# Rotary partner rows by on-chip transfers, and the last projection computed by token rows

## The reference, cut to what matters

```python
for layer in range(DEPTH):
    h = h + 0.5 * rms_norm(swiglu(rms_norm(h, g[0]), ffn_w_in[layer, 0], ffn_w_out[layer, 0]), g[1])
    hn = rms_norm(h, g[2])
    m = attention_mixer(...) if layer % 2 == 0 else recurrent_mixer(...)
    h = h + rms_norm(m, g[3])
    h = h + 0.5 * rms_norm(swiglu(rms_norm(h, g[4]), ffn_w_in[layer, 1], ffn_w_out[layer, 1]), g[5])
return h[:, N_META:]

def apply_rope(x, cos, sin):      # per head, after its RMS norm with gain
    x1, x2 = x[..., :32], x[..., 32:]
    return jnp.concatenate([x1 * c - x2 * s, x1 * s + x2 * c], axis=-1)
```

## Time and profile before

| | us |
|---|---|
| median of the runs shown (3) | 1121.16 |
| lowest, highest | 1120.73, 1124.25 |
| the profiled execution's own time | 1124.99 |
| its span, first to last instruction | 1123.2 |
| TensorE busy with products in it | 1074.9 (96%) |
| VectorE, ScalarE, GpSimd busy | 716.9, 552.4, 117.7 |
| mean granted TensorE clock | 0.987 of full speed |

### The profile page before, as it was taken

How to read it: one execution, slowest core, us unless ns; L and a number is a source line. 1 busy time by engine, 2 the same in 40 slices (tenths; PEclk the granted TensorE clock), 3 DMA queues, 4 the chain that set the end, 5 groups by cost and what they waited for, 6 DMA issues and landing times.

```text
span 1123.2 us, 21352 instructions
## 1 busy us (share of the span) xinstructions
PE 1074.9 (96%) x8696; PEld 1046.3 (93%) x8696; DVE 716.9 (64%) x1012; ACT 552.4 (49%) x806; POOL 117.7 (10%) x103
## 2 busy tenths in 40 slices
PE   6999999998899999999999999999997699999998
PEld 5999999987669999999999999999897699999997
DVE  5766655475574766664467666545889967666542
ACT  4544454452575544435454534534587455444541
POOL 2000000033100200000020000000477310000000
PEclk9999999998999999999999999999998899999999
DMA  8565446625103255445645454557153163645541
GB/s 245 192 202 169 133 148 201 230 76 160 39 1 113 82 193 176 150 155 169 211 141 187 152 173 154 162 185 225 56 171 125 33 217 125 214 153 174 179 131 38
DMA packets 166464, 169.65 MB, mean 151 GB/s; under 512 B 3312, under 2 KB 165416, under 8 KB 166392
## 3 DMA queue, kind: packets, MB, share of 16 engines
q1 hardware_dynamic: 166088, 168.16, 46.6%
q0 software_dynamic: 96, 0.28, 0.1%
q10 hardware_dynamic: 208, 0.20, 0.1%
HBM read 167.30 MB, written 1.05 MB: 150 GB/s over the span
## 4 chain that ended last, share of the span: by engine, by line
PE 85%; DVE 11%; issue 2%; ACT 2%; DMA 1%; POOL 0%; SPq 0%; DVEq 0%
PE bank L365 25%; PE bank L367 24%; PE bank L366 24%; DVE wl L1090 2%; DVE h L1133 1%; PE bank L393 1%; PE flipped L582 1%; DVE gm L1386 1%; PE weighed L594 1%; DVE mg L1129 1%; DVE xl L1096 1%; PE bank L373 1%; ACT wh L735 1%; PE bank L486 1%; PE bank L384 1%
## 5 line engine op out<-in xcount | busy, mean ns | idle before, releaser
L1090 DVE TENSOR_TENSOR wl<-raw,wh 128x2048 fp32r<-128x2048 f32 (+2 forms) x178 | 366.3, 2078 | 177.2 <-ACT wh L735 176.8
L365 PE MATMUL bank<-xh,wl 128*128 128x272 f32 (+1 forms) x1552 | 451.1, 291 | 10.4 <-DVE xl L1391 7.9
L367 PE MATMUL bank<-xh,wh 128*128 128x272 f32 (+1 forms) x1552 | 448.4, 289 | 0.0
L366 PE MATMUL bank<-xl,wh 128*128 128x272 f32 (+1 forms) x1552 | 446.9, 288 | 0.0
L735 ACT ACTIVATE wh<-raw 128x2048 fp32r<-128x2048 f32 (+2 forms) x177 | 299.3, 1714 | 97.3 <-PE bank L367 97.3
L365 PEld LDWEIGHTS bank<-xh,wl 128*128 128x128 f32 x1552 | 295.4, 190 | 13.0 <-DVE xl L1391 8.1
L366 PEld LDWEIGHTS bank<-xl,wh 128*128 128x128 f32 x1552 | 295.3, 190 | 0.1
L367 PEld LDWEIGHTS bank<-xh,wh 128*128 128x128 f32 x1552 | 295.3, 190 | 0.0
L365 PE MATMUL bank<-ah,wl 128*128 128x272 f32 (+1 forms) x704 | 201.5, 286 | 0.0
L367 PE MATMUL bank<-ah,wh 128*128 128x272 f32 (+1 forms) x704 | 201.1, 286 | 0.0
L366 PE MATMUL bank<-al,wh 128*128 128x272 f32 (+1 forms) x704 | 201.1, 286 | 0.0
(11 more groups left out here) (165 smaller groups left out, 1145.2 us busy)
## 6 DMA issues: line engine op xcount, KB each, us to landing
raw<-in_ffn_w_in SPq DMA_DIRECT2D x88, 1024.0 KB, 5.2
raw<-in_ffn_w_out SPq DMA_DIRECT2D x32, 768.0 KB, 5.1
raw<-in_ffn_w_out SPq DMA_DIRECT2D x32, 640.0 KB, 4.3
raw<-in_rec_w_in SPq DMA_DIRECT2D x8, 1024.0 KB, 5.4
raw<-in_attn_w_qkv SPq DMA_DIRECT2D x6, 1024.0 KB, 5.0
raw<-in_attn_w_o SPq DMA_DIRECT2D x4, 1024.0 KB, 5.2
raw<-in_rec_gate_w SPq DMA_DIRECT2D x16, 256.0 KB, 3.7
raw<-in_rec_w_out SPq DMA_DIRECT2D x4, 1024.0 KB, 5.7
```

The lines of the kernel that those rows point to most:

```text
L365: pe.matmul(dst, b, mh, start=first, stop=False)
L366: pe.matmul(dst, a, ml, start=False, stop=False)
L367: return pe.matmul(dst, a, mh, start=False, stop=last)
L1090: dve.tensor_tensor(wl[:, slot(u), 0:kn * 256], w, wh[:, slot(u), 0:kn * 256].bitcast(F32), ALU.subtract).then_inc(w_ready, 1)
```

## The change

1. `rotate` leaves TensorE. The matrix `rotm` goes. ScalarE issues four transfers per tile within on-chip memory, 32 partitions by 272 columns each (34 KB), that put each partition's partner row into `sqh`; the sign goes into the sine table. `times_sin` waits for them and reads `sqh` instead of PSUM.
2. The order of the query stage changes. On TensorE: `head_means(t-1)` behind chunk 3, `spread_scale(t-1)` behind the tile's products. On VectorE: for tile t-1 root-in, factor, sine and final all in iteration t, and at the end `final` of the last tile behind the first normalisation. ScalarE: `rotate(t)` behind `squared(t)`; those of tiles 0 and 1 stand ahead of the two first weight copies. GpSimd: `roped(t)` directly behind `times_cos(t)`.
3. Keys and values: for each chunk the two thirds of the products that need only the high part go first.
4. `keep_warm(3)` in `mean_of_projection` goes, at all places.
5. The last FFN's output projection has token rows as its result: the stationary operand is a block of 128 tokens of the hidden values, the moving one 512 columns of the weights. 2 halves of the channels, 2 token tiles, 22 chunks, 3 products each. Weights come in units of 4 chunks by 512 columns. The norm's sum of squares comes from ScalarE's square with accumulation, and gain, factor and residual are applied in token rows, the gain as a row vector spread over all partitions by a transfer. No spread product, no transposes at the end.
6. The residual `h` is therefore transposed to token rows during the last FFN's input part, in four groups of 4 transposes on TensorE (behind pairs 1, 2, 3 and 9), each copied from PSUM by ScalarE.

```diff
 def chunk(tiles, k, norm, t0, values=None, done=None):
     pe.wait_ge(xh_ready, KC * norm + k + 1)
     ...
+    if values is not None:
+        x, wv_h, wv_l, parts = values
+        for dst, a in parts:
+            pe.matmul(dst, x[:, k, a:a + KT], wv_l, start=k == 0, stop=False)
+            pe.matmul(dst, x[:, k, a:a + KT], wv_h, start=False, stop=False)
     pe.wait_ge(x_ready, KC * norm + k + 1)
@@ mean_of_projection
     last.then_inc(post_sum, 1)
-    keep_warm(3, bank[5])
     pe.wait_ge(rt_ready, pj + 1)
@@ TensorE, last FFN
+def turn_h(i):
+    t, half = divmod(i, 2)
+    if i:
+        pe.wait_ge(h_turned_copied, i)
+    for c in range(4):
+        last = pe.transpose(bank[6][:, c * P:(c + 1) * P], h[:, 4 * half + c, META + t * P:META + (t + 1) * P], ident)
+    last.then_inc(h_turned, 1)
+
+def last_out(f0):
+    def rows(half, t, j, k):
+        ...
+        th, tl = (v[:, f, META + t * P:META + (t + 1) * P] for v in (ah, al))
+        h512, l512 = (v[:, slot(u), 512 * k:512 * k + 512] for v in (wh, wl))
+        pe.matmul(dst, th, l512, start=f == 0, stop=False)
+        pe.matmul(dst, tl, h512, start=False, stop=False)
+        return pe.matmul(dst, th, h512, start=False, stop=f == FC - 1)
+    ...
@@ TensorE, query stage
         for k in range(KC):
             last = product(...)
-            if t == KT_N and k == 2:
+            if t == KT_N and k == 1:
                 pe.wait_ge(v_ready, 3)
                 head_means(0)
-                rotate(0)
-            if k == 4:
+            if k == 3:
                 head_means(t - 1)
-                rotate(t - 1)
-                if t > KT_N:
-                    spread_scale(t - 2)
-            if t == QKT - 1 and k == 4:
+            if t == QKT - 1 and k == 5:
                 pe.wait_ge(k_dup, 32)
                 scores(0)
         last.then_inc(qk_done, 1)
         if t == KT_N:
             spread_scale(0)
+        spread_scale(t - 1)
@@ ScalarE, query stage
+def rotate(t):
+    act.wait_ge(q_gained, t + 1)
+    if t >= 2:
+        act.wait_ge(q_sin, t - 1)
+    for a, b in ((0, 32), (32, 0), (64, 96), (96, 64)):
+        act.dma_start(sqh[a:a + 32, t % 2, :], qp[b:b + 32, t % 2, :]).then_inc(q_turned[t % 2], 16)
 squared(0)
 squared(1)
 root_of_h(1)
+rotate(0)
+rotate(1)
 act.wait_ge(v_done, 1)
 high(U_QKV + 4, 0)
 high(U_QKV + 5, 0)
 root(0)
 for t in range(KT_N, QKT):
     root(t - 1)
     squared(t)
+    rotate(t)
     if t % 2 and t < QKT - 1:
         high(U_QKV + 2 + (t - KT_N) // 2 + 4, 0)
@@ VectorE, query stage
-head_root_in(0)
-times_sin(0)
 for t in range(KT_N, QKT):
-    head_factor(t - 2)
-    head_root_in(t - 1)
-    times_sin(t - 1)
-    final(t - 2)
+    for u in (0, 1) if t == KT_N else (t - 1,):
+        head_root_in(u)
+        head_factor(u)
+        times_sin(u)
+    if t == KT_N:
+        final(0)
+    final(t - 1)
     ...
@@ VectorE, behind the last product
+for t in range(2):
+    gained(1, t)
+    dve.wait_ge(y_root, t + 1)
+    dve.reciprocal(yrt[:, t, 1:2], yrt[:, t, 1:2]).then_inc(y_factor, 1)
+    dve.wait_ge(y_factor, t + 1)
+    for half in range(2):
+        ...
+        dve.scalar_tensor_tensor(h_tok[:, t, cols], y_tok[:, t, cols], yrt[:, t, 1:2], h_tok[:, t, cols],
+                                 ALU.mult, ALU.add).then_inc(out_ready[t], 1)
@@ ScalarE, behind the last product
+for t in range(2):
+    squares(1, t)
+    act.wait_ge(y_sum, t + 1)
+    act.wait_ge(y_squared, 3 + t)
+    act.activation(yrt[:, t, 1:2], ysq[:, t, 1:2], ACT.Sqrt, scale=4.0 / D, bias=yrt[:, t, 0:1]).then_inc(y_root, 1)
```

More of the change, by code:

```diff
@@ L126, in shape_constants @@
         c[b * half:(b + 1) * half, C_COS:C_COS + L] = cos
-        c[b * half:(b + 1) * half, C_SIN:C_SIN + L] = sin
+        c[b * half:(b + 1) * half, C_SIN:C_SIN + L] = sin if b % 2 else -sin
     return c
@@ L267, in build, with last_bank @@
         ACC = 8
+        def last_bank(half, t):
+            return bank[(4, 2)[half] + t]
         def ffn_banks(m):
@@ L350, in _ @@
             ffn(3)
[L351 to L354, removed]
-                    sp.dma_start(out[t * P:(t + 1) * P, cols], tok_out[:, t, cols]).then_inc(s_out, 16)
+            for t in range(2):
+                for half in range(2):
+                    cols = slice(D // 2 * half, D // 2 * (half + 1))
+                    sp.wait_ge(out_ready[t], half + 1)
+                    sp.dma_start(out[t * P:(t + 1) * P, cols], h_tok[:, t, cols]).then_inc(s_out, 16)
             sp.wait_ge(s_out, 16 * 4)
@@ L373, in keep_warm, with chunk @@
                     pe.matmul(dst[:, 0:P], ident, ident, start=True, stop=True)
-            def chunk(tiles, k, norm, t0):
+            def chunk(tiles, k, norm, t0, values=None, done=None):
                 pe.wait_ge(xh_ready, KC * norm + k + 1)
@@ L382, in chunk @@
                     pe.matmul(dst, a, xh[:, k, t0:L], start=False, stop=False)
+                if values is not None:
[3 more added lines that the diff above has]
+                        pe.matmul(dst, x[:, k, a:a + KT], wv_h, start=False, stop=False)
                 pe.wait_ge(x_ready, KC * norm + k + 1)
-                return [pe.matmul(dst, wh[:, slot(u), tile * P:(tile + 1) * P], xl[:, k, t0:L], start=False, stop=k == KC - 1)
+                last = [pe.matmul(dst, wh[:, slot(u), tile * P:(tile + 1) * P], xl[:, k, t0:L], start=False, stop=k == KC - 1)
                         for dst, u, tile in tiles]
+                if done is not None and k == KC - 1:
+                    for product_done in last:
+                        product_done.then_inc(done, 1)
+                return last
             def spread(dst, cols, heads=1):
@@ L1133, in add @@
                     dve.tensor_tensor(h[:, c, t0:L], h[:, c, t0:L], mg[:, c, t0:L], ALU.add).then_inc(h_ready, 1)
[L1135 to L1147 removed]
+                for c in range(KC):
+                    scale(c)
+                    add(c)
+                    if c >= 1:
+                        low_x(n, c - 1)
+                low_x(n, KC - 1)
             def ffn(n, after):
@@ L1190, in pair @@
                         out_unit = 2 * p + j + 4 - FFN_IN_UNITS
[L1191 removed]
+                        low(u0 + 2 * p + j + 4, it, OUT_K[out_unit] if out_unit >= 0 and n < 3 else KC)
                 scaled(0)
```

218 lines of the change are left out of this document (137 added, 81 removed).

## The result

The changed kernel takes 1131.80 us (median of 7, 1129.17 to 1132.38), the kernel before beside it 1122.32 (7 runs, 1120.73 to 1124.85). The ratio is 1.0083, 95% interval 1.0070 to 1.0097: slower by some 9.5 us, where 1119.8 was forecast, and outside the range of 1113 to 1126. Profiled execution: 1131.93, span 1130.1, mean granted clock 0.970 (before: 1124.99, 1123.2, 0.987).

The account below looks back on a forecast made before the run. TensorE, holding 85% of the chain, was taken as the bound. Tail -6.8, turning h +3.2, wide products -2.5, fillers elsewhere -0.6 and query stage +5.3 made -1.4: median 1119.8 us from 1121.16, range 1113 to 1126.

Parts of the forecast that it names:

- The tail: After the last product: serial work to the end of the span falls from 12.57 to 5.7 us, -6.8.
- Turning h: Last FFN's input part: 16 added transposes cost TensorE in full, 0.8 us for each of four groups, +3.2.
- Wide products: Last output projection: 264 products of 512 columns at 225 ns replace 528 of 256, -2.5 us taken.
- keep_warm(3): Ends of projections: removing three fillers between sums and spread gains 0.15 us at each of five places, -0.75.
- K and V: Keys and values: TensorE starts with the high half, ready earlier than the low half, -0.8 us.
- The query stage: Query stage: rotation product removed, transfers issued by ScalarE, three long waits with clock falls; +5.3 us, K and V included.
- four issues: Query stage: a tile's four transfers at 0.45 us each hold ScalarE's queue for 1.8 us.
- landing: Query stage: rotation transfers land 2.1 us after the last issue, with 5.0 kept as bound.
- Rival C: Query stage: transfers land late (5.0 us) and ScalarE's queue holds the roots; +6.5, 1126 us, chance 0.15.
- B: Query stage loses nothing, clock holds or falls only twice; 1113 to 1116 us, say 1114.5, chance 0.25.
- D: Last output projection: 512-column products gain nothing or a little less (236 ns); 1122.3 us, chance 0.10.
- E: Last output projection: 512-column products cost exactly their columns (213.3 ns), -6 in place of -2.5; 1116.3 us, chance 0.05.

Follow-up runs that it names:

- the kernel with fillers: Changed kernel with filler products of 128 columns added in TensorE's waits in the query stage; 1123.24 us, ratio 0.9999 to the kernel before.
- The dose of 8, 4, 2 and 0: Changed kernel with eight half-size, four, two (others by GpSimd) or no (all GpSimd) transfer issues per tile on ScalarE: ratios 1.0274, 1.0083, 1.0013, 0.9970.
- the tenth: Changed kernel with all rotation transfers issued by GpSimd, fillers in TensorE's remaining waits and item 4 undone; 1117.27 us, ratio 0.9968.
- order-only kernel: Kernel before with item 2 alone, the rotation kept as a product on TensorE, no transfers; 1118.28 us, ratio 0.9963.

## Why the prediction was wrong, step by step

**The tail** was forecast at 5.7 and takes 5.35; 7.2 is gained for 6.8. **Turning h** was forecast at 0.8 a group and costs 0.43, 1.7 in all for 3.2: the four transposes take 0.35 (959.41 to 959.76) for 0.56, and the switch between the kinds of product 0.08 for 0.2. **Wide products:** 0.231 for 0.225; 264 make 61.0 against 62.3, so -1.3 for -2.5. By the Trainium skill ("TensorE: Matmul & The Clock Gate", Back-to-back issue gap) it would have been 0.216, which is its figure for a product alone; the 0.231 of the trace differs, and decides. The two errors nearly cancel: the FFN before the tail came out at +0.67, and +0.7 was the sum of the two steps. That is luck. By the rows the two make +0.4, and the other 0.3 is in none of them.

**keep_warm(3)** (-0.75): from the first sum to the spread's start it is 2.08 at the first place in place of 2.22, the 0.15 of the forecast, but 0.46 of it is idle now, and the clock falls behind it. Nothing is left. **K and V** (-0.8): -0.6 in their own part where item 3 stands alone, and more than lost in the wait that follows; in the changed kernel, with the low clock from 225 to 230, they take 0.15 more than before. Both steps failed in the same way. I priced the engine's own time and not the idle time that the edit makes ahead of the next wait, though the earlier trace rows showed a fall behind each wait of 2.4; a wait of 1.43 that left the clock alone made me think short waits safe.

**The query stage** failed (+5.3 for +12.7). To compare positions I add to those of the changed kernel the 0.67 by which its execution is ahead at the end of the first FFN.

| | forecast | measured |
|---|---|---|
| four issues | 1.8 | 2.44 |
| landing | 2.1 | 2.6 |
| root(0) | 250.9 | 252.8 |
| product 3 | 254.65 | 257.0 |
| waits, tiles 3, 4, 5, 7 | 0.65, 0, 3.0, 3.1 | 1.41, 0.35, 3.53, 3.94 |
| last product ends | 298.9 | 304.7 |
| second turn | 306.4 | 313.6 |

- The start is 2.35 later than forecast. 1.5 of it are eight issues at 0.61 to 0.64 in place of 0.45. 0.4 comes from K and V, behind which the first issue starts at 244.0 for 243.6. The rest is the clock in the two spreads: from spread(0) to product 3 it is 3.50 for a forecast of 3.10 (2.99 in the kernel with fillers, at full clock). Tile 2 ran at 1.2 GHz too, from the longer wait before the head means on, for which I had charged nothing; but it ended inside the wait for root(0) and moved nothing: measured from the end of K and V, spread(0) starts at 10.1 here and at 10.1 with the fillers and a full clock.
- The waits of tiles 3, 4, 5 and 7 are 2.5 longer together, about the 0.64 of issue time each.
- Another 1.0 up to the last product is, by what is left, clock: 1.9 was charged behind each long wait, and behind the last of them it was 0.50 from 294.7 to about 304.
- 1.4 more behind the last product: issues ahead of the last root, and the clock at 0.50 again from 308 to 314, behind the wait of 1.98, with scores and the first turns in it. How the 1.4 divide is not shown.

Together 7.25 of the 7.4 that were missing. The step that failed first is the price of an issue, taken from issues at the start of the program: it makes 4.0 of the 7.4 by the first two points. The dose of 8, 4, 2 and 0 shows that the mechanism (ScalarE's queue ahead of roots and weight copies) was the right one. The clock's part was also undersized: three falls at 1.9 and 0.5 for the start of the attention steps were charged, 6.2, and filling the waits gives 7.7.

Rival C, on the right side, had the wrong place: its landing of 5.0 was 2.6, and VectorE waited 0.2 for it. It was found in the kernels with issues by GpSimd, where the landings cost 7.8 and 10.7. B, D and E are out. What none of them had: items 1 and 2 have opposite signs, -3.8 for the order and +16.6 for the transfers in place of the product. I forecast them as one sum, so the order's worth and the product's cheapness stayed hidden.

**Not foreseen and not explained:** the recurrent stage's 1.4, a fall of the clock from 819.6 on behind a wait of 1.8 which the kernel before has too (1.81, ended at 806.5) with the clock at 1.00 behind it. The layout is excluded as the cause. The transfers go with it in nine of ten profiles and are not enough for it, by the tenth. It stays open.

## What to carry to other kernels

An operation of 0.64 on the busiest engine may be cheaper than four issues of 0.61 on a half idle one, if that one's queue feeds the busiest engine: count issues in the queue they stand in, at the price of such issues in the middle of the program. Price an edit on TensorE with the wait that it leaves behind: where the clock falls behind waits, work saved ahead of a wait can cost more than it saves, and a few fillers in that wait keep the gain. Forecast an order and a replaced operation apart, and if they can be run apart, do.

## What the runs showed of the hardware that I had not expected

- An issue of a transfer within on-chip memory costs ScalarE 0.61, for 32 partitions and for 16 alike; GpSimd issues the same one in 0.50.
- The clock fell to 1.2 GHz behind idle times of 0.46 (item 4 alone, at five of six places) and 1.38 (item 3 alone), while in the order-only kernel it held behind 0.86 twice; so the length of a wait alone does not decide.
- Four transposes between products cost 0.43 on TensorE, the switch only 0.08 of it. Products of 512 columns are 0.231 apart, those of 256 were 0.118: some 2% less per column.
